# Splitting the projection's operands inside the mixer stage, and adding squares one job later, in a two-network transformer kernel

## The reference, cut to what matters

```
def heads_out(att, p, hy, w_out):
    f = fourier_mix(p[..., OFF_F:OFF_H])
    hz = hyena_mix(p[..., OFF_H:], *hy)
    return jnp.concatenate([att, f, hz], axis=-1) @ w_out
...
        x = x + g1 * heads_out(att_x, px, hy, w_out[l])
        x = x + g2 * sq_relu_mlp(modulate(rms_norm(x, norm2_g[l]), sh2, sc2), w_mlp1[l], w_mlp2[l])
        if not last:
            ...
            xc = xc + cg1 * heads_out(att_c, pc, hy, w_out[l])
```

## Time and profile before

| | |
|---|---|
| median of 3 runs | 3476.98 us (3476.12 to 3478.43) |
| the profiled execution | 3477.29 us |
| its span in the trace | 3475.5 us, mean granted clock 0.977 |
| PE busy | 3302.2 us, 95% of the span |
| DVE busy | 2004.7 us, 58% |
| ACT busy | 1312.6 us, 38% |
| DMA | 356.13 MB, mean 102 GB/s |

### The profile page before, as it was taken

One profiled execution on the slowest core, in us unless ns is written; L12 is line 12 of the kernel. 1 busy time (PEld: TensorE's weight loads), 2 busy tenths in 40 slices (PEclk: granted clock), 3 DMA queues, 4 the chain that ended last, 5 costly groups with the idle time before them and its releaser, 6 DMA issues.

```text
span 3475.5 us, 42655 instructions
## 1 busy us (share of the span) xinstructions
PE 3302.2 (95%) x17650; PEld 2726.4 (78%) x17650; DVE 2004.7 (58%) x2797; ACT 1312.6 (38%) x1949; POOL 58.4 (2%) x59
## 2 busy tenths in 40 slices
PE   7898989999999998999989999999899999889998
PEld 3685567888888755988887888888888888788887
DVE  6677666777556476565557656333654555563333
ACT  3324445232234245533354545222533333362223
POOL 0000000000000000000000010000100000020000
PEclk8899999999999999999999999999999999999998
DMA  5541022545444220365532222332243333123221
GB/s 176 171 128 63 13 73 75 174 147 156 154 153 133 85 77 13 113 194 183 175 91 61 80 67 85 99 101 92 55 102 80 73 90 80 58 81 101 97 97 49
DMA packets 375408, 356.13 MB, mean 102 GB/s; under 512 B 73471, under 2 KB 320558, under 8 KB 373807
## 3 DMA queue, kind: packets, MB, share of 16 engines
q1 hardware_dynamic: 374995, 353.32, 33.3%
q10 hardware_dynamic: 220, 0.07, 0.0%
HBM read 345.50 MB, written 4.72 MB: 101 GB/s over the span
## 4 chain that ended last, share of the span: by engine, by line
PE 50%; DVE 5%; ACT 3%; issue 1%; DMA 0%; POOL 0%; SPq 0%; DVEq 0%; ACTq 0%; POOLq 0%
PE ps L403 45%; PE ps L2714 1%; DVE r_st L2597 1%; PE ps L2735 1%; DVE second_w_lo L570 1%; ACT second_w_hi L511 1%; PE ps L2724 1%; ACT second_scr L712 0%; PE ps L2737 0%; DVE sums L487 0%; DVE x_res L896 0%; DVE second_scr L894 0%; DMA ring<-in_ffn_w_in 0%; POOL sq L470 0%; PE ps L2443 0%
## 5 line engine op out<-in xcount | busy, mean ns | idle before, releaser
L403 PE MATMUL ps<-second_h_hi,second_w_hi 128*128 128x512 f32 (+1 forms) x2216 | 823.1, 371 | 35.4 <-DVE second_h_lo L922 14.9
L403 PE MATMUL ps<-second_h_hi,second_w_lo 128*128 128x512 f32 (+1 forms) x2216 | 809.3, 365 | 0.0
L403 PE MATMUL ps<-second_h_lo,second_w_hi 128*128 128x512 f32 (+1 forms) x2216 | 808.6, 365 | 0.0
L570 DVE TENSOR_TENSOR second_w_lo<-ring,second_w_hi 128x2048 fp32r<-128x2048 f32 (+2 forms) x176 | 373.7, 2123 | 458.5 <-ACT second_w_hi L511 458.4
L403 PEld LDWEIGHTS ps<-second_h_hi,second_w_hi 128*128 128x128 f32 x2216 | 427.8, 193 | 101.7 <-issue 20.1
L403 PEld LDWEIGHTS ps<-second_h_hi,second_w_lo 128*128 128x128 f32 x2216 | 427.1, 193 | 65.6
L403 PEld LDWEIGHTS ps<-second_h_lo,second_w_hi 128*128 128x128 f32 x2216 | 427.8, 193 | 61.4
L511 ACT ACTIVATE second_w_hi<-ring 128x2048 fp32r<-128x2048 f32 (+2 forms) x176 | 311.6, 1771 | 269.8 <-PE ps L403 263.3
L403 PE MATMUL ps<-h_mix_hi,w_hi 128*128 128x512 f32 (+2 forms) x776 | 270.5, 349 | 15.0 <-DVE h_mix_lo L1013 6.4
L403 PE MATMUL ps<-h_mix_lo,w_hi 128*128 128x512 f32 (+2 forms) x776 | 267.3, 344 | 0.0
L403 PE MATMUL ps<-h_mix_hi,w_lo 128*128 128x512 f32 (+2 forms) x776 | 266.9, 344 | 0.0
(11 more groups left out here) (451 smaller groups left out, 5420.5 us busy)
## 6 DMA issues: line engine op xcount, KB each, us to landing
ring<-in_w_mlp SPq DMA_DIRECT2D x64, 1024.0 KB, 5.4
side_w<-in_ada_w SPq DMA_DIRECT2D x96, 512.0 KB, 4.8
ring<-in_ffn_w_in SPq DMA_DIRECT2D x44, 1024.0 KB, 5.1
side_w<-in_w_mod SPq DMA_DIRECT2D x80, 512.0 KB, 3.8
ring<-in_attn_w_in SPq DMA_DIRECT2D x48, 512.0 KB, 5.2
ring<-in_hgrn_w_in SPq DMA_DIRECT2D x32, 512.0 KB, 4.8
ring<-in_ffn_w_out SPq DMA_DIRECT2D x16, 1024.0 KB, 5.0
ring<-in_w_in SPq DMA_DIRECT2D x14, 1024.0 KB, 5.5
```

The costliest lines, as they stand in the source:

```text
L403: mm = pe.matmul(acc, lhsT, rhs, start=k == 0 and wp == ap, stop=k == j.kt - 1 and wp == 1)
L570: dve.tensor_tensor(unit.place(unit.slot[1]), unit.place(M.ring[:, u % RING, :]), unit.place(unit.slot[0]), ALU.subtract).then_inc(*S.w_lo ...
```

## The change

1. `mixers` gets a `SplitAheadThread`. It splits the projection's weight unit 0 and seven of the eight mixed blocks while the last heads are attended. On ACT the seven high parts stand behind the attention's pieces of units 16 to 22 in layer 0 (10 to 15 in layer 1), the weights' high part behind the exponent of item 39 (27). On DVE the weights' low part stands at unit 20.5 (14.25), the seven low parts at half units from 21 to 24 (14 to 16.25).
2. The buffers of the hand-over in layer 0 get fixed places (`SplitApart`), where the mixers' own buffers are dead by then.
3. The region of the projection (`R.ahead = 1`) leaves out the split of unit 0 and waits one less on the counts of split units; only block 13 is split there. The first job takes the blocks in `OUT_ORDER`, with block 13 at its last place.
4. DVE adds a job's squares (`add_squares`) in the turn of the next job, behind that job's evacuation, except for the last job of a half (`closes`) or of a run of squared jobs.
5. In the tails of the first network the second half's jobs are `slow`: the low part of a unit whose slot came free is made one job later.
6. A `BorderThread` of the second half (not the last one) puts its sums at `start + 2.3` on PE, one job later.

```diff
+        self.closes, self.order = False, None
...
             if u >= RING:
                 yield max(self.freed(v) for v in range(u - RING + 1))
-                sp.wait_ge(S.w_lo.sem, S.w_lo.at(u - RING + 1))
+                sp.wait_ge(S.w_lo.sem, S.w_lo.at(u - RING + 1 - self.ahead))
...
-        for k in range(k0, 0 if j.make else k1):
+        for at in range(k0, 0 if j.make else k1):
+            k = j.order[at] if j.order else at
...
-        self.high(act, 0)
+        if not self.ahead:
+            self.high(act, 0)
...
+    def add_squares(self, dve, j):
+        S, M, n = self.S, self.M, j.n
+        _, dst, fresh = j.square
+        dve.wait_ge(S.sq_act.sem, S.sq_act.at(j.square_nth + 1))
+        if fresh:
+            dve.engine_nop().then_inc(*S.sq_add.one)
+        else:
+            dve.tensor_tensor(dst, dst, M.sq[:, 0, 0:n], ALU.add).then_inc(*S.sq_add.one)
...
-        self.low(dve, 0)
+        if not self.ahead:
+            self.low(dve, 0)
...
-            if j.square and not j.by_pool:
...
+            for other in squares:
+                self.add_squares(dve, other)
+            squares = [j] if j.square and not j.by_pool else []
+            if squares and (j.closes or not (j.at + 1 < len(self.jobs) and self.jobs[j.at + 1].square)):
+                self.add_squares(dve, j)
+                squares = []
             while u < len(self.units) and self.freed(u) <= j.at - j.slow:
                 self.low(dve, u)
...
-        yield self.start + 1.3
+        yield self.start + (1.3 if a == 0 or self.last else 2.3)
...
+class SplitAheadThread(Thread):
...
+        self.w = LX if X.last else T
+        self.mixes = 2 if X.last else 4
+        self.projections = 16 if X.last else 20
...
+    def weights_high(self, act):
...
+        act.activation(self.unit.place(self.slot[0]), self.unit.place(M.ring[:, 0, :]), ACT.Copy).then_inc(*S.w_hi.one)
...
+    def weights_low(self, dve):
...
+        dve.wait_ge(S["head_roped"].sem, S["head_roped"].at(HEADS))
+        dve.wait_ge(S.w_hi.sem, S.w_hi.at(1))
...
+    def scalar(self, act):
...
+            if k < 4:
+                act.wait_ge(S.stored.sem, S.stored.at(2 * X.per_head * (k + 1)))
+            act.activation(self.h.hi[:, k, 0:self.w], self.block(k), ACT.Copy).then_inc(*S["ahead_hi"].one)
...
+    def vector(self, dve):
...
+            dve.wait_ge(S.scores.sem, S.scores.at(2 * X.per_head * (HEADS - 1)))
+            dve.wait_ge(S["ahead_hi"].sem, S["ahead_hi"].at(n + 1))
+            dve.tensor_tensor(self.h.lo[:, k, 0:self.w], self.block(k), self.h.hi[:, k, 0:self.w],
+                              ALU.subtract).then_inc(*S["ahead_lo"].one)
...
+OUT_ORDER = (4, 5, 6, 7, 0, 1, 2, 3)
...
+        unit_at = lambda u, inside: T0 + u * W + inside
+        if both:
+            plan = zip(OUT_ORDER, (16, 17, 18, 19, 20, 21, 22), (21, 21.5, 22, 22.5, 23, 23.5, 24))
+            weights_at = unit_at(19.5, 5.1), unit_at(20.5, 2.9)
+        else:
+            plan = zip(OUT_ORDER, (10, 11, 12, 13, 14, 14.5, 15), (14, 14.5, 15, 15.5, 15.75, 16, 16.25))
+            weights_at = unit_at(13.5, 5.1), unit_at(14.25, 2.9)
+        threads.append(SplitAheadThread(X, units[0], slot, h, [(k, unit_at(a, 4.9), unit_at(b, 2.9)) for k, a, b in plan],
+                                        weights_at))
...
+        R.ahead = 1
...
-                    at = R.add(*on(units[c], mark(out_jobs(c, [g], split, evac))))
+                    jobs = mark(out_jobs(c, [g], split, evac))
+                    for j in jobs:
+                        j.slow = g == both[1]
+                    at = R.add(*on(units[c], jobs))
+                R.jobs[at].closes = True
                 yield g, at
...
-        mixed = SplitThread(R, [(k, M.p[:, b, 0:hi]) for k, b in enumerate((10, 11, 12, 13, 6, 7, 8, 9))], h, 0, hi, -1)
+        mixed = SplitThread(R, [(OUT_ORDER[-1], M.p[:, 13, 0:hi])], h, 0, hi, -1)
...
-                jobs[0].ready = mixed.needs()
+                jobs[0].ready, jobs[0].order = mixed.needs(), OUT_ORDER
```

More of the change, by code:

```diff
@@ L402, in products @@
                 lhsT, rhs = ops if j.weights_first else ops[::-1]
-                mm = pe.matmul(acc, lhsT, rhs, start=k == 0 and wp == ap, stop=k == j.kt - 1 and wp == 1)
-            if k < k1 - 1:
-                yield base + share * (k + 1 - k0) / (k1 - k0)
+                mm = pe.matmul(acc, lhsT, rhs, start=at == 0 and wp == ap, stop=at == j.kt - 1 and wp == 1)
+            if at < k1 - 1:
+                yield base + share * (at + 1 - k0) / (k1 - k0)
         if k1 == j.kt and hi == j.n:
@@ L625, in _ @@
                 for u, unit in enumerate(ahead):
-                    sp.wait_ge(self.S.w_lo.sem, self.S.w_lo.at(len(self.units)))
+                    sp.wait_ge(self.S.w_lo.sem, self.S.w_lo.at(len(self.units) - self.ahead))
                     for to, src in unit.pieces(self.M.ring[:, u, :]):
@@ L2085, in sync, with __init__, block @@
         X.M.loaded = len(self.units)
-def mixers(nc, S, M, io, l):
+class SplitAheadThread(Thread):
+    def __init__(self, X, unit, slot, h, blocks, weights_at):
+        self.X, self.unit, self.slot, self.h, self.blocks, self.weights_at = X, unit, slot, h, blocks, weights_at
+        self.w = LX if X.last else T
+        self.mixes = 2 if X.last else 4
+        self.projections = 16 if X.last else 20
+    def block(self, k):
+        return self.X.M.p[:, (10, 11, 12, 13, 6, 7, 8, 9)[k], 0:self.w]
+    def weights_high(self, act):
+        X, S, M = self.X, self.X.S, self.X.M
+        act.wait_ge(S.weights[0].sem, S.weights[0].at(1))
+        act.wait_ge(S["hyena_out"].sem, S["hyena_out"].at(self.mixes))
+        act.wait_ge(S["head_acc"].sem, S["head_acc"].at(self.projections))
+        act.activation(self.unit.place(self.slot[0]), self.unit.place(M.ring[:, 0, :]), ACT.Copy).then_inc(*S.w_hi.one)
+    def weights_low(self, dve):
+        X, S, M = self.X, self.X.S, self.X.M
+        dve.wait_ge(S["head_acc"].sem, S["head_acc"].at(self.projections))
+        dve.wait_ge(S["head_roped"].sem, S["head_roped"].at(HEADS))
+        dve.wait_ge(S.w_hi.sem, S.w_hi.at(1))
+        dve.tensor_tensor(self.unit.place(self.slot[1]), self.unit.place(M.ring[:, 0, :]), self.unit.place(self.slot[0]),
+                          ALU.subtract).then_inc(*S.w_lo.one)
+    def scalar(self, act):
+        X, S = self.X, self.X.S
+        done = False
+        for k, at, _ in self.blocks:
+            if at > self.weights_at[0] and not done:
+                yield self.weights_at[0]
+                self.weights_high(act)
+                done = True
+            yield at
+            act.wait_ge(S["hyena_out"].sem, S["hyena_out"].at(self.mixes))
+            act.wait_ge(S["fourier_out"].sem, S["fourier_out"].at(self.mixes))
+            if k < 4:
+                act.wait_ge(S.stored.sem, S.stored.at(2 * X.per_head * (k + 1)))
+            act.activation(self.h.hi[:, k, 0:self.w], self.block(k), ACT.Copy).then_inc(*S["ahead_hi"].one)
+        if not done:
+            yield self.weights_at[0]
+            self.weights_high(act)
+    def vector(self, dve):
+        X, S = self.X, self.X.S
+        done = False
+        for n, (k, _, at) in enumerate(self.blocks):
+            if at > self.weights_at[1] and not done:
+                yield self.weights_at[1]
+                self.weights_low(dve)
+                done = True
+            yield at
+            dve.wait_ge(S["hyena_out"].sem, S["hyena_out"].at(self.mixes))
+            dve.wait_ge(S["head_acc"].sem, S["head_acc"].at(self.projections))
+            dve.wait_ge(S.scores.sem, S.scores.at(2 * X.per_head * (HEADS - 1)))
+            dve.wait_ge(S["ahead_hi"].sem, S["ahead_hi"].at(n + 1))
+            dve.tensor_tensor(self.h.lo[:, k, 0:self.w], self.block(k), self.h.hi[:, k, 0:self.w],
+                              ALU.subtract).then_inc(*S["ahead_lo"].one)
+        if not done:
+            yield self.weights_at[1]
+            self.weights_low(dve)
@@ L2090, in mixers @@
+OUT_ORDER = (4, 5, 6, 7, 0, 1, 2, 3)
+def mixers(nc, S, M, io, l, h, slot):
     with ExitStack() as ctx:
@@ L2196, in first_layer @@
                 R.emit(nc)
-    mixers(nc, S, M, io, l)
     hi = outer[-1][1]
+    if last:
+        h, hid, slots = B.h, B.hid1, B.slots
+    else:
+        kb = lambda n: M.base + int(1024 * n)
+        h = SplitApart(nc, f"h_mix{l}", [P, KD, hi], kb(44), kb(0))
+        hid = SplitAt(nc, f"hid{l}", [P, KD, hi], M.slab)
+        slots = [SplitApart(nc, f"w_mix{l}_{i}", [P, SLOT], kb(a), kb(b)).parts for i, (a, b) in enumerate(((68, 86), (24, 32)))]
+    mixers(nc, S, M, io, l, h, slots[0])
     first, second = (C_COLS, X_COLS) if l == 0 else ((0, LX // 2), (LX // 2, LX))
@@ L2226, in first_layer @@
     with ExitStack() as ctx:
[L2227 to L2234 removed]
+        if not last:
+            M.scr = [nc.alloc_sbuf_tensor_at(f"scr{l}_{i}", [P, 1024], F32, offset=kb(n))[:, :] for i, n in enumerate((40, 94))]
```

(8 more changed lines are left out.)

44 lines of the change are left out of this document (18 added, 26 removed).

## The result

The changed kernel takes 3458.27 us (median of 4 runs, 3454.52 to 3461.08), the kernel before 3476.55 in the same comparison (4 runs): a ratio of 0.9949, 95% interval 0.9937 to 0.9960.

What follows compares the result with a forecast made beforehand. PE, busy 95% of the span, was taken as the bound. Hand-overs 14.7, less attention 3.8 and 5.3, plus tails 2.1, border sums 0, gave 7.7 us: 3477.0 - 7.7 = 3469.3 us, range 3460 to 3477.

Steps and rivals of the forecast that it cites:

- The hand-overs: Mixers to projection, both layers: PE starts 5.2 and 4.9 us earlier, clock losses of 2.9 and 1.7 go; 14.7 won.
- the clock's 2.9: Hand-over of layer 0: 14 matmuls take 6.08 us instead of 3.2 at the lower clock; this 2.9 us loss goes.
- Attention of layer 0: Split work inserted in DVE's and ACT's queues makes the mixers end 3.8 us later (bounds 0 and 8.5).
- it starts some 2.7 us late: Layer 0's attention: DVE's maximum at 457.67 starts 2.7 us late; the delay then grows to about 3.8.
- Attention of layer 1: Low part delays a maximum 3.5 us, PE waits about 3.4, clock falls (1.7); 5.3 us paid.
- Rival (c): TensorE's clock falls in both layers' attention, staying low until the projection; slower, 3488 us; chance 0.07.
- Tail 1: Projection of layer 0, tail of 541.24: later squares and `slow` win 0.8 us.
- Tail 2: Second tail of layer 0 (MLP): later squares and `slow` win about 1.0 us.
- tail 3: Projection of layer 1, tail of 1444.31: the sum comes 1.6 us later, of which PE pays 0.6.
- tail 4: Entry, tail of 1812.50: sum 1.8 us sooner, last low part before the recurrence's first steps; 0.9 won.
- Border sums: Second network's borders: the wait moves behind the jobs; 0 us (bounds 2 won, 1 lost).
- rival (a): The attention hides the inserted work; hand-overs bring 14.7 less about 2, tails as forecast; 3462 us; chance 0.25.

Runs made afterwards that it cites:

- b3: The changed kernel with the weights' low part one step sooner on DVE in both layers; 3457.72 us, 0.9946 of the kernel before.
- b4: The changed kernel with the weights' low part one step sooner in both layers and border sums at start + 1.3; 3459.83 us, 0.9951 of the kernel before.
- c1: The changed kernel with the weights' low part one step sooner in layer 1 alone; 3456.37 us (0.9938 of the kernel before), run again 3452.06 us (0.9932).
- a3: The changed kernel without `slow` in the first network's tails; 3467.68 us, 0.9978 of the kernel before.
- a2: The changed kernel with squares added in their own job's turn again; 3470.54 us, 0.9983 of the kernel before.
- a4: The kernel before with the later squares, `slow` and the later border sums, but no split ahead; 3473.52 us, 0.9990 of the kernel before.
- a1: The changed kernel with squares in their own turn, nothing new slow, border sums at start + 1.3; 3467.00 us, 0.9974 of the kernel before.
- b2: The changed kernel with the border sums at start + 1.3 again; 3459.23 us, 0.9949 of the kernel before.

## Why the prediction was wrong

**The hand-overs were right** to 0.1 us: 8.03 and 6.55 against 8.1 and 6.6, with PE's gap of 1.21 and the clock at 1.00, in every profile of the changed kernel. But b3 and b4 show that the clock's 2.9 is not safe: they gave 1.6 of it back behind a gap of the same length. And the reason given, that the clock had stayed at 1.00 through the attention's gaps of this size, was read from the end of the attention only: at 344 to 346 us the kernel before had gaps of 1.19 and 0.99 us, with a clock of 0.50 behind them. That it held at this hand-over was not certain from the rows.

**Attention of layer 0: 3.8 forecast, 1.62 measured.** The sign and the place were right. The step that failed is the item-by-item chain from "it starts some 2.7 us late" on: the maximum was 1.9 late; PE lost 0.5 us by 458.5 (times of before), 1.0 more by 463 and 0.1 behind that. The chain itself said that a low part (0.88) and the attention (1.7) make 2.6, which is the pace; a delay does not grow then, and the 1.1 added for growth was wrong.

**Attention of layer 1: 5.3 forecast, 4.42 measured.** The mechanism is shown, by b3, b4, and both profiles of c1: the low part's place ahead of the maximum. PE waited 2.60 rather than 3.4, and the clock fell as assumed. It cost 1.65, the difference to a3, against the 1.7 assumed. It was also avoidable, one step higher in DVE's order. The fall came in eight of nine profiles with that wait and in none of the four with 0.71 in its place. Rival (c), a fall in layer 0 too that lasts until the projection, did not come: 1.00 there from 380 us on. The Trainium skill's rule that the prediction weighed ("TensorE: Matmul & The Clock Gate", A second HAM failure mode: psum-queue depth-cycling), that many small gaps can make the clock swing, was not borne out where the split work stands. The fall to 0.50 at 346 us, in the kernel before as in the changed one, agrees with it; so the prediction's "the rows at 1.00 disagree" holds only for the rows that it read.

**Tail 1: 0.8 forecast, 4.35 measured.** This is the largest miss, 3.5 us. The step "three waits of 0.5 go and 0.5 comes back, later the low part is wanted just then" looked at the sum's row alone. It left out the wait of 1.49 us for a weights' low part 15 us earlier, which the additions on DVE delay by way of ACT, and the four waits around the second norm, which the pair of squares and `slow` ends. a2, a3 and a4 show both. Tail 2 (1.0 against 1.34), tail 3 (0.6 lost against 0.70) and tail 4 (0.9 against 0.4 to 1.5) were near. For tail 2 that is luck: its waits did not shrink, its clock was better. For tail 3 a1 shows that the reason need not be the one given, and the third profile of the unchanged kernel lost 1.4 us there.

**Border sums: 0 forecast**, nothing beyond 1 us shown (b2). The wait did move behind the jobs, as said: 1.91 + 5.93.

**The sum.** What repeats in all profiles of the changed kernel is 8.03 + 6.55 - 1.62 - 4.42 + 4.35 + 1.34 - 0.70 + 0.43 to 1.51 = 14.0 to 15.0 us, 6 to 7 more than forecast, by tail 1 (3.5), layer 0's attention (2.2), layer 1's (0.9) and small ones. That alone would give 3462 to 3463 us, inside the range and near rival (a)'s 3462, but in another way: the attention did pay, 6.0 us where 9.1 were forecast. The median gained 18.3, and the 3 to 4 us left put it below the range. No profile locates them: the mean spans of three profiles of each kernel differ by 15.8 us only. What moves by 1 us or more between profiles of the changed kernel is the first 450 us, the Fourier mix, tail 4, the borders and the last 30 us. Three profiles a kernel can't say whether the change makes good outcomes there more frequent; this stays open. The range had no term for it.

## What to carry to other kernels

Where an engine's queue is fixed, look for every wait that stands behind the removed one, not for the largest alone: additions that each waited half a microsecond also held, by way of ACT, a weights' low part 15 us upstream of the sum, and the second half of the gain came only with the edit that alone lost time. Put inserted work in front of an instruction that waits anyway (1.94 us of idle took 2.29 us of work and left PE 0.71 to wait), not in front of one that another engine waits for. And set the n-th matmul of one trace against the n-th of the other, over more than one profile of each: it shows which microseconds repeat. Split each difference into idle time and pace: tail 2 gained what was forecast, and none of it by the waits that the edits were to remove.

## What was not expected of the hardware

Behind a gap the granted clock is not the same from one execution to the next. The Fourier mix of layer 1, the same instructions behind the same gap, took 26.0, 26.0 and 29.9 us in three profiles of the changed kernel, with the clock at 1.00 in the second and 0.58 in the third over the stretch shown; the third profile of the kernel before lost 1.4 us in tail 3 and won 1.5 and 1.7 at the second border and the end against the first. The Trainium skill says of the window in which the chip looks at PE's activity that it is free-running and does not start with the kernel ("TensorE: Matmul & The Clock Gate", What's actually happening). These profiles agree with that in so far as the same program meets different clocks at the same gap; that the window is the cause, they don't show. Other outcomes repeated in all three profiles of the changed kernel: the low clock behind the wait of 2.60 us in layer 1's attention (0.83 in the stretch shown), and the 1.00 behind the 1.21 us of both hand-overs. Neither is a rule of the gap's length: a3 kept 1.00 behind 2.59 us, b3 had 0.87 and 0.85 behind 1.20, and both kernels had 0.50 behind 1.2 and 0.99 in layer 0.
